# Two transformer blocks in one launch: w_ada sums, convolution order, weight splits and the last stage of a hand-ordered kernel

## The reference

```python
mod = jax.nn.silu(c) @ w_ada[l] + b_ada[l]
shift1, scale1, gate1, shift2, scale2, gate2 = jnp.split(mod[:, None, :], 6, axis=-1)
h = rms_norm(x, norm1_w[l]) * (1 + scale1) + shift1
proj = h @ w_in[l]
...
qkv = jax.nn.silu(causal_dwconv(jnp.concatenate([dn_q, dn_k, dn_v], axis=-1), dn_conv_w[l]))
o_a = gated_delta_rule(q_a, k_a, v_a, g_a, beta_a)
y_a = (rms_norm(o_a, dn_norm_w[l]) * jax.nn.silu(dn_z)) @ w_out_dn[l]
y_b = mla_attention(...) @ w_out_mla[l]
mix = jax.nn.sigmoid(gate_dn) * y_a + jax.nn.sigmoid(gate_mla) * y_b
x = x + gate1 * (mix @ w_o[l])
h2 = rms_norm(x, norm2_w[l]) * (1 + scale2) + shift2
x = x + gate2 * ((gelu(conv(a_path)) * v_path) @ ffn_w_down[l])
```

```python
ple_gate = jax.nn.sigmoid(jnp.einsum('bsd,de->bse', hg, w_ple_gate[i]) + b_ple_gate[i])
h = h + ple_gate * jnp.einsum('bsq,qd->bsd', p[i], w_ple[i])
return rms_norm_2(h, final_g)
```

## Time and profile before

| | us |
|---|---|
| median of 3 runs | 2433.01 |
| the three runs | 2432.54, 2433.01, 2443.62 |
| the profiled execution | 2446.43 |
| its span in the profile | 2444.5 |
| TensorE's mean granted clock in it | 0.973 of full |

### The profile page before, as it was taken

One profiled execution on the slowest core, in us unless ns is written; L12 is line 12 of the kernel. 1 busy time (PEld: TensorE's weight loads), 2 busy tenths in 40 slices (PEclk: granted clock), 3 DMA queues, 4 the chain that ended last, 5 costly groups with the idle time before them and its releaser, 6 DMA issues.

```text
span 2444.5 us, 26836 instructions
## 1 busy us (share of the span) xinstructions
PE 2339.8 (96%) x10936; PEld 1872.6 (77%) x10936; DVE 1097.0 (45%) x1600; ACT 932.0 (38%) x1352; POOL 673.4 (28%) x399
## 2 busy tenths in 40 slices
PE   8899999999999999999999899999999999999996
PEld 3678889876666787788888788778777787888875
DVE  2677665534533433533321689623453242332233
ACT  2564442124434333433332332345553343332334
POOL 1133234000311244222223213221232353332333
PEclk9899999999999999999999999999999999999998
DMA  8332121411222132433333433232212332333331
GB/s 274 119 117 73 46 61 35 121 35 35 76 56 56 59 112 87 129 96 94 103 95 95 129 95 95 70 91 82 78 60 62 121 95 79 111 95 95 104 121 52
DMA packets 347984, 220.65 MB, mean 90 GB/s; under 512 B 18394, under 2 KB 327245, under 8 KB 347861
## 3 DMA queue, kind: packets, MB, share of 16 engines
q1 hardware_dynamic: 338462, 202.31, 28.2%
q10 hardware_dynamic: 9398, 16.62, 2.0%
HBM read 210.49 MB, written 8.41 MB: 90 GB/s over the span
## 4 chain that ended last, share of the span: by engine, by line
PE 82%; DVE 7%; ACT 6%; issue 2%; POOL 2%; DMA 1%; ACTq 0%; SPq 0%; DVEq 0%; POOLq 0%
PE ps L343 80%; ACT arena L361 2%; DVE arena L372 2%; DVE scr L372 1%; PE ps L346 1%; DVE arena L364 1%; ACT whi L361 1%; ACT scr L361 1%; POOL arena L364 1%; ACT L352 1%; DMA ada_late<-in_w_ada_dram 1%; POOL wlo L364 1%; ACT L361 0%; POOL hlo L364 0%; DVE scr L364 0%
## 5 line engine op out<-in xcount | busy, mean ns | idle before, releaser
L364 POOL TENSOR_TENSOR wlo<-wraw,whi 128x1024 fp32r<-128x1024 f32 (+1 forms) x163 | 391.1, 2400 | 1158.3 <-ACT whi L361 1158.3
L343 PE MATMUL ps<-hhi,whi 128*128 128x512 f32 x1664 | 452.3, 412 | 35.1 <-ACT whi L361 24.2
L361 ACT ACTIVATE whi<-wraw 128x1024 fp32r<-128x1024 f32 (+1 forms) x328 | 340.9, 1040 | 336.6 <-PE ps L343 285.3
L343 PE MATMUL ps<-hlo,whi 128*128 128x512 f32 x1664 | 424.5, 394 | 1.3 <-POOL hlo L364 1.2
L343 PE MATMUL ps<-hhi,wlo 128*128 128x512 f32 x1664 | 421.2, 392 | 0.9 <-POOL wlo L364 0.9
L343 PEld LDWEIGHTS ps<-hhi,whi 128*128 128x128 f32 x1664 | 317.6, 195 | 121.0 <-issue 44.1
L343 PEld LDWEIGHTS ps<-hlo,whi 128*128 128x128 f32 x1664 | 318.4, 191 | 70.8 <-POOL hlo L364 2.1
L364 DVE TENSOR_TENSOR wlo<-wraw,whi 128x1024 fp32r<-128x1024 f32 (+2 forms) x165 | 216.8, 1314 | 334.7 <-ACT whi L361 334.4
L343 PEld LDWEIGHTS ps<-hhi,wlo 128*128 128x128 f32 x1664 | 314.5, 189 | 68.4 <-POOL wlo L364 2.6
L343 PE MATMUL ps<-arena 128*128 128x128 f32 (+6 forms) x2304 | 331.7, 298 | 17.2 <-ACT arena L361 9.6
L343 PEld LDWEIGHTS ps<-arena 128*128 128x128 f32 (+1 forms) x2304 | 282.2, 195 | 46.8 <-issue 19.6
(11 more groups left out here) (194 smaller groups left out, 2546.2 us busy)
## 6 DMA issues: line engine op xcount, KB each, us to landing
wraw<-in_w_in_dram SPq DMA_DIRECT2D x99, 512.0 KB, 3.8
wraw<-in_w_ff_dram SPq DMA_DIRECT2D x64, 512.0 KB, 3.9
wraw<-in_ffn_w_up_dram SPq DMA_DIRECT2D x44, 512.0 KB, 3.8
wraw<-in_w_gate_dram SPq DMA_DIRECT2D x32, 512.0 KB, 3.5
arena<-in_w_ada_dram SPq DMA_DIRECT2D x22, 512.0 KB, 3.8
arena<-in_w_ada_dram SPq DMA_DIRECT2D x8, 1024.0 KB, 11.5
wraw<-in_ffn_w_down_dram SPq DMA_DIRECT2D x16, 512.0 KB, 3.5
wraw<-in_w_branch_dram SPq DMA_DIRECT2D x16, 512.0 KB, 3.4
```

Of the source, the lines that this page charges most:

```text
L343: return pe.e.matmul(o, l, r, start=start, stop=stop)
L361: return ac.e.activation(o, i, f, bias=bias, scale=scale, **kw)
L364: return q.e.tensor_tensor(o, a, b, op)
```

## The change

It has these parts.

- **Prologue.** The row products are gone. VectorE multiplies and adds row blocks of w_ada in the layout in which they land (24 operations of 128 x 512, `mod_part` of Vector), TensorE takes 5 and 3 of the 32 row blocks itself and sums the rest over the partitions, both by matmuls of one column (28 and 20, `mod_part` and `mod_sum` of Tensor). Four of the copies of x and all scalings of h go from VectorE to ScalarE (`first_h`). x tiles 4 to 7 are turned between the steps of the first batch.
- **Qkv head.** `ev_ab` runs the convolutions of its two blocks without the flush; `gates_ab` has two more empty steps on ScalarE and on VectorE; the w_ada steps start at the third unit.
- **Recurrence.** `adas` ends with part 4; the recurrence has no w_ada steps beside those of the projections. Part 5 runs in `ffn1`, a step after each odd g. `NEAR` is 20.
- **Splits.** `split_to(name, n)` splits up to the n-th unit of a product. It stands ahead of the last `mix` rounding (wo), between the first k steps of `norm2` (ple and fu0), where the ple steps of ScalarE come later, ahead of the SiLU of the conv branch (aq) and of sv_norms (su), and at the third head of the linear attention's norm (wg10). `ev_yb` rounds one tile later.
- **Last stage.** Adding and squaring of tile m come with tile m + 1 on VectorE and ScalarE (`pg_add`), the turn of tile m with m + 3; GpSimd multiplies up to tile 6; the last tile is VectorE's, and is turned into two banks from `FN`, scaled straight to `OUT`. The sum of squares comes in two parts (`rt`, `rt7`). The table load stands behind the last sigmoid.

Core of the diff, in the order of the code (constants; class Stages; program; Tensor's batch, `mod_part`, `between`, `ev_pg`; Scalar's prologue, `first_h`, `gates_ab`, `ev_yb`, `norm2`, `conv`, `sv_norms`, gated linear attention, `ev_pg`; Vector's `mod_part`, `ada_add`, `norm2`):

```diff
-        ADA_ROW = [A[0:1, 53 + p, :] for p in range(2)]
+        ADA_PE = [[(1, 3, 5, 7), (7,)], [(3, 7), (7,)]]
...
-        NEAR = 22
+        NEAR = 20
...
+            def split_to(self, name, n):
+
+                self.ahead(W.index[L[name].units(L[name].batches()[0][0])[0][0]] + n - 3)
...
-                    self.kept.append((8 * m - 8, bk))
-                    self.conv_kept()
+                    self.dn_conv(8 * m - 8, bk)
+                    self.dn_taps(8 * m - 8, bk)
+                    self.due.append(8 * m - 8)
...
-                    next(more, None)
+                    if n > 1:
+                        next(more, None)
...
-                for p in range(2, 6):
+                for p in range(2, 5):
...
+                last = self.ada(5)
...
+                    if g % 2:
+                        next(last, None)
...
-            weave(paced(f.mla_proj(), more), paced(f.recur(), more), 8, 16)
+            weave(paced(f.mla_proj(), more), f.recur(), 8, 16)
...
+            f.yb_end()
...
+                            if l.X is H1 and k == 4:
+                                lows(3)
+                                self.between(4)
+                                highs(4)
+                                continue
...
+            def mod_part(self, bk, s, p, g):
+                for k in ADA_PE[s][p]:
+                    if k // 4 == g:
+                        pe.wait_ge(SG.sem(f"ada_in{s}{p}{g}"), 16)
+                        for c in range(4):
+                            mm(bk[:, 4 * p + c:4 * p + c + 1], ADA0[s][p][:, k, c * P:(c + 1) * P], SC[:, k:k + 1],
+                               not self.opened, False)
+                            self.opened = True
...
+                if k in (1, 2, 3):
+                    self.turn_x(3 + k)
                 if k == 4:
-                    self.ada_half(1)
+                    self.turn_x(7)
+                    bk = self.mod_open(1)
+                    self.mod_part(bk, 1, 0, 0)
+                    self.mod_part(bk, 1, 0, 1)
+                    self.mod_part(bk, 1, 1, 0)
+                    self.mod_sum(bk, 1, 0)
+                    self.mod_part(bk, 1, 1, 1)
+                    self.mod_sum(bk, 1, 1)
...
-                if m >= 2:
-                    self.turn(m - 2)
+                if m >= 3:
+                    self.turn(m - 3)
...
+                self.ahead(-2)
+                self.ahead(-1)
+                self.first_h(0)
                 self.ahead(0)
-                for k in range(8):
+                for k in range(1, 8):
...
+                act(HS[k % 3], PA.of("hx", k)[:, :], ACT.Identity, bias=modcol(0, k), scale=modcol(1, k)).then_inc(
+                    *inc("st_act", "h", k))
+                ac.wait_ge(*at("st_act", "h", k))
+                self.high(H1, k, HS[k % 3])
...
             def gates_ab(self):
+                yield
...
             def ev_yb(self, m, bk):
+                ac.wait_ge(*at(*lin_end("ya")))
+                if m:
+                    self.mix_high(m - 1)
+
+            def mix_high(self, m):
                 ac.wait_ge(*at("mix_po", m))
-                ac.wait_ge(*at(*lin_end("ya")))
                 self.high(HM, m, MIX[m])
+
+            def yb_end(self):
+                self.split_to("wo", 2)
+                self.mix_high(7)
...
-                    if k % 2:
+                    if k == 0:
+                        self.split_to("ple", 4)
+                    elif k < 3:
+                        self.split_to("fu0", k)
+                    if k in (2, 5):
                         next(extra, None)
+                run(extra)
...
+                self.split_to("aq", 3)
...
+                self.split_to("su", 3)
...
+                    if h == 2:
+                        self.split_to("wg10", 1)
...
+                if m == 7:
+                    self.pg_add(6)
+                    self.turn(4)
                 ac.wait_ge(*at("pg_ve", m))
                 act(sc, sc, ACT.Sigmoid, bias=col("bp", m)).then_inc(*inc("pg_act", m))
+                if m == 7:
+                    load_log_exp()
+                elif m:
+                    self.pg_add(m - 1)
+                if 3 <= m < 7:
+                    self.turn(m - 3)
+
+            def pg_add(self, m):
                 ac.wait_ge(*at("x4_ve", m))
-                for p in SG.ends("9"):
-                    ac.wait_ge(*p)
-                act(FN[m], XR[m], ACT.Copy, scale=col("mf", m)).then_inc(*inc("fn_act", m))
-                self.square("pg", m, XR[m], [A[:, 32, :], A[:, 33, :]], lambda m: "po" if m < 6 else "ve")
-                if m >= 2:
-                    self.turn(m - 2)
+                if m < 7:
+                    for p in SG.ends("9"):
+                        ac.wait_ge(*p)
+                    act(FN[m], XR[m], ACT.Copy, scale=col("mf", m)).then_inc(*inc("fn_act", m))
+                self.square("pg", m, XR[m], [A[:, 32, :], A[:, 33, :]], lambda m: "po")
...
+            def mod_part(self, s, p, g, only=range(8)):
+                o = ADA0[s][p][:, 0, :]
+                mine = [k for k in range(8) if k not in ADA_PE[s][p]]
+                for k in mine:
+                    if k // 4 == g and k in only:
+                        ve.wait_ge(SG.sem(f"ada_in{s}{p}{g}"), 16)
+                        if k == 0:
+                            ve.wait_ge(*at("st_act", "sc"))
+                            t = ts(ve, o, o, SC[:, 0:1], None, ALU.mult)
+                        else:
+                            ve.wait_ge(*last("m0_ve"))
+                            t = stt(o, ADA0[s][p][:, k, :], SC[:, k:k + 1], o, ALU.mult, ALU.add)
+                        t.then_inc(*(inc("m0_ve", s, p) if k == mine[-1] else inc("m0_ve")))
...
+                if p == 5 and k == 0:
+                    ve.wait_ge(SG.sem("pls_out0"), 64)
+                    ve.wait_ge(SG.sem("pls_out1"), 64)
...
-                    if k % 2:
+                    if k in (1, 3, 5, 7):
                         next(extra, None)
+                    if k == 2:
+                        self.split_to("fu0", 2)
```

236 lines of the change are left out of this document (144 added, 92 removed).

## The result

| | us |
|---|---|
| changed kernel, median of 4 runs | 2371.06 (2368.69 to 2371.84) |
| kernel before, median of the 4 runs beside them | 2436.94 (2432.54 to 2443.62) |
| ratio, with its 95% interval | 0.9725 [0.9705, 0.9744] |
| profiled execution after (before) | 2371.21 (2446.43) |
| its span after (before) | 2369.4 (2444.5) |

What follows compares the result with a forecast made beforehand. TensorE's own time was taken as the bound. Terms summed to 73.1 us, less 6 for uncovered stalls: 67.1; from the median 2433.0, leaving out 12.0 of half clock, this gave 2378 (2355 to 2403).

Steps and rivals of the forecast that it cites:

- net sum: All gains, 73.1 us, less 6 for uncovered stalls: 67.1 from the profiled run; 12.0 less from the median.
- C: Recurrence: TensorE's wait for VectorE and the half clock behind it go; 16 us (3 to 16.4), 4.4 for the median.
- A: Prologue: sums on VectorE replace row products, so TensorE's first batch starts and ends earlier; 17.5 us (11 to 20).
- the price to 0: Prologue: VectorE's sums slowed beside two GpSimd `wlo`; taken as 0, with 4.2 us at most kept in the bound.
- the rival of the clock: Prologue's small matmuls leave the first batch at half clock, the recurrence's stretch back too: 2405 to 2412; chance 0.09.
- B: Head of the qkv convolutions: 7.9 us of idle time and 3.1 of low clock go; 11 us (6 to 16).
- the slower side's rival: w_ada steps in the FFN wait for loads and hold TensorE; at 9 us each 2459; chance 0.04.
- D: Splits ahead of ScalarE's waits: 6.2 us before wo, 7.2 before the FFN, 1.9 at aq, 3 at wg10.
- the half that I gave it: At wg10, 3 us of a possible 6.1, because its `wlo` is GpSimd's, behind work that isn't moved.
- F: Last stage: 2.5 us of `whi` waits and 7.8 of tail behind the last product go; 10.3 us (7 to 12).
- The allowance: Taken off the whole sum: 0.5 us for each of a dozen places where a removed stall uncovers the next, 6.

Runs made afterwards that it cites:

- the second trace: The kernel before, unchanged, traced a second time: median 2436.1 of 10 runs (2432.2 to 2439.9), ratio 0.9993; its profiled execution took 2435.6.

## Why the prediction was right, and where its steps were off

**The baseline.** The prediction started from a median of three runs, 2433.0. The 27 further runs of the kernel before that were taken beside the experiments have medians of 2438.0, 2438.4 and 2439.1, its ten of the second trace 2436.1. Against 2438 the change brought 66.9 us; the net sum for the profiled run was 67.1, the one for the median 55.1. That 67.1 and 66.9 agree is partly luck: the sum was made for the pair of profiled runs, and these differ by 75.1. The step that took C's 12 us of half clock out of the median was wrong: that stretch is in both traces of the kernel before, where it cost 12.0 and 4.6, and the profiled execution was longer at other places too, by about as much. It made the forecast 12 us too high, the low baseline made it 5 too low, and the 7 us are what was left.

**A, 17.5 forecast, 14.2 in the traces, 13.7 undone.** The first batch started at 29.9 and not at 28. The prediction had the factors at 24.8; with 0.7 and 0.6 behind them that makes 26.1, and it wrote 27.7, so 1.6 us stood in it without a name. In the trace the last sum ends at 23.9, not 22.7, the factors would be there at 26.3 without GpSimd, and are there at 28.2. The earlier trace rows had shown that GpSimd holds VectorE up, and the prediction put the price to 0, "which counts only where VectorE is last": it did count, since not a long sum but the four-column one on the path met GpSimd. VectorE lost 1.9 us by it and TensorE 0.8, because ScalarE's second `whi` would have held up the first h until 27.5, its load being there 1.15 us later than in the kernel before. In seven of the eleven traces with this prologue TensorE's one-column matmuls at half clock were last; there the first batch starts at 30.9 to 31.3, in the four others at 29.2 to 29.9. The second half started at 50.5 and not at 46 to 47. The 20 one-column matmuls (42.08 to 48.5) took 6.4 us, for which the prediction's price of 0.23 each gives 4.6; the last 16 of their 40 passes ran at a clock of 0.50, 1.84 for eight, and behind them VectorE's and ScalarE's steps take 2.0. That is the rival of the clock in small. (the earlier trace rows is misread too: a row counts passes, two for each matmul, so these are four matmuls, at a clock of 0.50 in 2430 to 2436. At full clock twice as many take the same time, so that the price came out right.)

**B, 11 forecast, 11.6 and 11.7.** One wait of 3.40 stayed, forecast 3.1. A second, 2.03 for VectorE at 118.28, was not forecast; the recovered clock (0.95 for 0.88) paid for it: of idle time 5.6 us went, not the 7.9 of the forecast, and of half clock 0.12 x 85.6 - 0.05 x 73.8 = 6.6, not 3.1.

**C, 16 forecast for the profiled run, 17.8 and 17.5.** The size was right for the pair of traces; the 4.4 that the prediction put for the median is what failed, since undoing this part alone costs 17.5 in the median. Of the half clock, see above. No w_ada load made VectorE wait in the FFN, and TensorE's idle time in 372 us there is 0.9: the slower side's rival did not come up. A pair of sums took 2.68 us there, not 1.42, and that didn't hold TensorE either.

**D, 13.4 forecast for wo and norm2, 11.9 + 1.84 moved in = 13.7, and 13.7 by the starts of the kernel with the splits undone.** The wait for the even unit's `wlo`, 0.7 forecast, is 0.84 at 936.97. aq gave 2.0 (1.9). wg10 gave 1.3, forecast 3, and -1.5 against the kernel with the splits undone: the `wlo` of GpSimd took the place of ScalarE's `whi` in full, 2.67 for 2.71, and only the half clock behind it varied. The mechanism was named and the half that I gave it was too much. With the wait itself removed the place gave 4.5 more in the traces, 5.8 in all, near the 6.1 that the earlier trace rows had given.

**F, 10.3 forecast, 12.2 and 12.0.** Behind the last product the tail is 2369.4 - 2355.6 = 13.8 (13.5 forecast, 21.3 before). Inside the stage 4.7 us went, not 2.5: TensorE's idle time there fell from 3.6 to 0, the wait for the turn (1.10) among it, which had no term, and its busy time fell by 1.1, in part because the turn of one tile now comes behind the last product. The table load:

```profile
2357.28 1.28 ACT L352 ACT_TABLE_LOAD   x1
2358.75 0.63 ACT L361 ACTIVATE arena<-arena 128x512 f32<-128x512 f32 x1 [0.18 <-DVE arena L364]
```

It ends at 2358.56, and the square behind it waits another 0.18 for VectorE, not for the load. Nor is there a gap ahead of the load: the sigmoid ends at 2357.26. By the drain of 1380 ns that the Trainium skill adds to a switch (ScalarE: Activation LUTs, What ACT_TABLE_LOAD costs), the square could not have started ahead of 2359.9. It started 1.2 us earlier.

**The allowance** of 6 us for waits that are uncovered was about right in the waits (2.03 in the head, 2.69 at 1764.51 where there were 0.38; the 2.67 at wg10 stands in a term of its own), but half clock that went at places with no term, 3.0 and 1.6 in the table of starts, made up for it. The row at 1764.51 is the instructive one. In the kernel before, TensorE was at half clock ahead of it (0.5 in 1815 to 1825), so it came later and waited 2.3 us less. There ScalarE and VectorE set the pace, not TensorE, and a clock that comes back buys nothing: the longer wait took the gain, half clock now stood behind the row (0.5 in 1765 to 1770), and the lead fell from 63.8 to 61.6 us.

## What to carry to other kernels

Where TensorE is busy 96% of the time, price a wait at about twice its length, because half clock mostly follows it (4.07 cost 8.5, 2.67 cost 4.5; one of 2.71 drew none at all); but only where TensorE is the one that others wait for. When a split, a table load or a sum stands behind a wait in an engine's own order, move it ahead of the wait on every engine that has a part in it: moved on ScalarE alone, wg10 gave 1.3 us in one pair of traces and -1.5 in another, moved on GpSimd and for ScalarE's next unit too it gave 4.5 more. When one lock or one late result is blamed for a late start, look at what the next engine was doing meanwhile: VectorE lost 1.9 us in the prologue, and the batch only 0.8. And take a trace of the same kernel twice before one execution's half-clock stretches are put into a sum: here the two differed by 11 us.

## What the runs showed of the hardware

A VectorE instruction can be stopped for the whole of a GpSimd one, however small it is: 4 columns took 2.04 us beside a `wlo` of 2.35 and 0.16 without. The operation just ahead, 8 columns of which one input comes from the accumulator (`ps`), ran beside the same `wlo` in 0.17. Scalings of 512 columns from `ada_late` suffer too, 1.8 and 1.5 us in the FFN, beside a `wlo` (957.69 to 960.09) and a product of GpSimd, where 0.48 is usual:

```profile
958.58 3.23 DVE L368 TENSOR_SCALAR scr<-ada_late,mod 128x512 f32<-128x512 f32 x2
```

It goes both ways: two `wlo` back to back beside two `hlo` took 6.07 us, where they are 4.7 alone; with the two `hlo`, 0.69 each, that makes 6.1. The Trainium skill (SBUF — State Buffer, SBUF: two separate sides) calls this an exclusive lock: the one that starts first has the shared ports for its whole instruction. The rows of 2.04 and 2.35 agree: 26.16 + 2.04 is 25.82 + 2.35 to 0.03 us.

The half clock that follows a wait varies between executions of one kernel: behind the same wait of 4.4 to 4.7 us it cost 12.0 in one and 4.6 in the other. Behind the wait of 2.71 at wg10 the clock was 0.77 over 15 us in the kernel before and 1.00 with the splits undone.
